# Two transformer blocks on one core: block one's attention heads computed by feature, sums and silu of block two placed elsewhere, other PSUM banks

## The reference

```python
mix = jnp.concatenate([y_m, y_b, y_n], axis=-1)          # 512 + 256 + 256 features
x = x + jnp.einsum('bse,ed->bsd', mix, w_out[l])
h = rmsnorm(x, norm_ffn[l])
u = jnp.square(jax.nn.relu(jnp.einsum('bsd,df->bsf', h, w_ff1[l])))
x = x + jnp.einsum('bsf,fd->bsd', u, w_ff2[l])
...
return gj[:, 0] * o_c + gj[:, 1] * o_s + gj[:, 2] * o_w   # nsa, per token and head
```

## Time and profile before

| | |
|---|---|
| median of 3 runs | 1090.6 us (1089.24 to 1091.53) |
| profiled execution, its time | 1088.39 us |
| its span | 1086.6 us |
| mean granted clock of TensorE | 0.997 of full |
| PE busy | 1064.1 us, 98% |
| DVE, ACT, POOL busy | 741.4, 618.6, 80.8 us |
| HBM read | 176.90 MB, 164 GB/s |

### The profile page before, as it was taken

One profiled execution on the slowest core, in us unless ns is written; L12 is line 12 of the kernel. 1 busy time (PEld: TensorE's weight loads), 2 busy tenths in 40 slices (PEclk: granted clock), 3 DMA queues, 4 the chain that ended last, 5 costly groups with the idle time before them and its releaser, 6 DMA issues.

```text
span 1086.6 us, 16764 instructions
## 1 busy us (share of the span) xinstructions
PE 1064.1 (98%) x6396; PEld 908.1 (84%) x6396; DVE 741.4 (68%) x1296; ACT 618.6 (57%) x1039; POOL 80.8 (7%) x96
## 2 busy tenths in 40 slices
PE   8999999999999999999999999999999999999997
PEld 7898888888888988888888887898987778989876
DVE  5889777677667888787766675684465657844554
ACT  6776754344436768563444354855656548556562
POOL 1010110000000100110000000004011000040120
PEclk9999999999999999999999999999999999999999
DMA  9853365555657534446566654654444456544432
GB/s 320 268 153 118 99 189 182 190 173 187 211 183 216 168 112 133 123 151 208 162 207 198 191 160 147 197 156 136 120 150 136 136 156 194 156 131 123 155 118 76
DMA packets 89404, 179.04 MB, mean 165 GB/s; under 512 B 8989, under 2 KB 20637, under 8 KB 89325
## 3 DMA queue, kind: packets, MB, share of 16 engines
q1 hardware_dynamic: 88605, 176.58, 52.1%
q10 hardware_dynamic: 720, 1.40, 0.4%
HBM read 176.90 MB, written 1.05 MB: 164 GB/s over the span
## 4 chain that ended last, share of the span: by engine, by line
PE 79%; DVE 8%; ACT 6%; issue 4%; DMA 3%; SPq 0%; DVEq 0%; POOL 0%; ACTq 0%; POOLq 0%
PE bank L852 18%; PE bank L854 17%; PE bank L853 17%; PE bank L918 11%; PE bank L920 5%; DVE w_lo L1824 2%; DMA raw<-in_w_in 2%; PE bank L1004 2%; ACT w_hi L1405 2%; PE bank L953 2%; PE bank L1061 1%; PE bank L1038 1%; DVE vecs L1833 1%; PE bank L1027 1%; PE bank L1333 1%
## 5 line engine op out<-in xcount | busy, mean ns | idle before, releaser
L1824 DVE TENSOR_TENSOR w_lo<-raw,w_hi 128x1024 fp32r<-128x1024 f32 (+1 forms) x319 | 385.7, 1221 | 228.1 <-ACT w_hi L1405 225.4
L1405 ACT ACTIVATE w_hi<-raw 128x1024 fp32r<-128x1024 f32 (+1 forms) x319 | 330.7, 1052 | 181.9 <-PE bank L854 96.7
L918 PE MATMUL bank<-h_parts,w_hi 128*128 128x512 f32 x512 | 180.7, 396 | 1.0 <-DVE arena L2201 0.7
L852 PE MATMUL bank<-h_parts,w_hi 128*128 128x256 f32 x512 | 149.3, 292 | 0.0
L853 PE MATMUL bank<-h_parts,w_hi 128*128 128x256 f32 x512 | 144.7, 283 | 0.0
L854 PE MATMUL bank<-h_parts,w_lo 128*128 128x256 f32 x512 | 144.6, 282 | 0.0
L852 PE MATMUL bank<-w_hi,h_parts 128*128 128x512 f32 (+1 forms) x352 | 141.2, 401 | 3.2 <-DVE w_lo L1866 2.0
L920 PE MATMUL bank<-h_parts,w_lo 128*128 128x256 f32 x512 | 143.4, 280 | 0.0
L853 PE MATMUL bank<-w_lo,h_parts 128*128 128x512 f32 (+1 forms) x352 | 136.5, 388 | 0.0
L854 PE MATMUL bank<-w_hi,h_parts 128*128 128x512 f32 (+1 forms) x352 | 136.5, 388 | 0.0
L918 PEld LDWEIGHTS bank<-h_parts,w_hi 128*128 128x128 f32 x512 | 96.0, 188 | 24.8 <-issue 2.6
(11 more groups left out here) (295 smaller groups left out, 1523.3 us busy)
## 6 DMA issues: line engine op xcount, KB each, us to landing
raw<-in_w_in SPq DMA_DIRECT2D x143, 512.0 KB, 3.8
raw<-in_w_ff SPq DMA_DIRECT2D x128, 512.0 KB, 4.3
raw<-in_w_out SPq DMA_DIRECT2D x40, 512.0 KB, 3.4
raw<-in_w_in SPq DMA_DIRECT2D x8, 404.0 KB, 5.5
xn<-in_cmp_w SPq DMA_DIRECT2D x8, 256.0 KB, 5.4
x_sb<-in_x SPq DMA_DIRECT2D x2, 512.0 KB, 9.1
mix<-in_cmp_w SPq DMA_DIRECT2D x4, 256.0 KB, 4.0
gain<-in_cmp_w SPq DMA_DIRECT2D x4, 256.0 KB, 5.6
```

The source lines that it names most:

```text
L852: pe.matmul(out_ap, s_hi, m_hi, start=start, stop=False, **kw)
L918: pe.matmul(ps[:, :].rearrange("p (a t) -> p a t", a=2), hi[:, kk, f], h_parts[:, :, k, :], start=k == 0, stop=False, skip_group_check=True)
L1405: act.activation(slot(w_hi, u), slot(raw, u), ACT.Copy).then_inc(hi_ready, 1)
L1824: dve.tensor_tensor(slot(w_lo, u), slot(raw, u), slot(w_hi, u).bitcast(F32), ALU.subtract)\
```

## The change

1. `BY_FEATURE` has "att1" too. In block one V runs once for a pair of heads, at the odd head's step, through `value_pair`; heads 0 to 3 accumulate in one use of bank 7, heads 4 to 11 in another. A stage N is added for each pair, at the end of step `start[h]` (the pair's S): DVE inverts the sums, times the gate for nsa (three instructions, two for moba); POOL scales the weights of both heads; T waits for POOL. `epilogue1` (three times a layer), the additions of its parts and `mix_turn` 2 and 3 are gone; after V of heads 3 and 11 ACT and DVE write `mixT1_hi`, `mixT1_lo` straight from bank 7.
2. `cmp_o` is computed transposed and added in bank 7; DVE's addition is gone.
3. Banks: the norms of the feed-forward use 4 to 7; `ff1(0)` uses banks 0, 1, 2, 4 and `ff1(1)` banks 5, 6, 7, 3.
4. The tail of the output projection waits for `mix_turn` 0 first and for `mix_turn` 1 only ahead of feature chunk 2.
5. Block two: `gate_silu` goes to the start of its step; `mix_full` to 33, 38, 48, 52; `mix_hi` to the start of 36, 39, 50, 53, and `mix_lo` one step after each; K of stick into the step of Z; the diagonal factor of the norm (L1885) from p = 5 to p = 4.

```diff
-BY_FEATURE = ("fox",)
+BY_FEATURE = ("att1", "fox",)
...
-        use(("norm", n, i, u), 2 * i if n in FFN_NORMS and u else 4 + 2 * u + i)
+        use(("norm", n, i, u), 4 + 2 * u + i)
...
-                for h in range(12):
+                for h in range(stage == "V", 12, 2 if stage == "V" else 1):
...
-                if p == 25:
-                    single(2, "mix_turn", 0, l, 2)
...
+                for h in range(0, 12, 2):
+                    if start[h] == p:
+                        head_steps(("att1", l), h, "N", 4)
...
-                use(("ff1", l, t, c), 4 + c)
+                use(("ff1", l, t, c), ((0, 1, 2, 4), (5, 6, 7, 3))[t][c] if t < 2 else 4 + c)
...
+            if p in (33, 48):
+                step("gate_silu", l, p // 48)
+            for n, turn_at in enumerate((36, 39, 50, 53)):
+                if p == turn_at:
+                    step("mix_hi", l, n)
+                if p == turn_at + 1:
+                    step("mix_lo", l, n)
...
-            for stage, lag in (("V", 3), ("R", 2), ("K", 1), ("Z", 0)):
+            for stage, lag in (("V", 3), ("R", 2), ("Z", 0), ("K", 0)):
...
+            if p in (33, 38, 48, 52):
+                step("mix_full", l, (33, 38, 48, 52).index(p))
...
+                    elif kind == "att1" and s[2] == "N":
+                        scale_weights("att1", l, s[3])
...
+                        elif s[2] == "N":
+                            g, r = divmod(s[3], 4)
+                            gate = n_gate[:, :, s[3]:s[3] + 2].rearrange("p i h -> p h i") if g else None
+                            row_inverses("att1", l, s[3], gate)
+                        elif s[2] == "V" and s[3] in (3, 11):
+                            g = s[3] // 8
+                            turned(("att1", l, "O", g), mixT1_hi[1][:, 2 * g:2 * g + 2, :], mixT1_lo[1][:, 2 * g:2 * g + 2, :])
```

More of the change, by code:

```diff
@@ L335, in hybrid_blocks @@
                 if p == 27:
-                    single(3, "cmp_o", l)
+                    step("cmp_o", l)
                     m_scores(0, 2)
@@ L351, in hybrid_blocks @@
             if p == 28:
-                single(7, "mix_turn", 0, l, 3)
                 m_values(0, 6)
@@ L429, in side2 @@
                 step("stats", 4 + l)
+            if p == 4:
+                step("r_diag", 4 + l)
             if p == 5:
@@ L933, in out_unit_products, with tail_products @@
                 return mm
-            def tail_products(name, a, features, turned_inside=()):
+            def tail_products(name, a, features, turned_inside=(), second_half=None):
                 for n, (f, hi_f, lo_f) in enumerate(features):
+                    if f == second_half:
+                        drained(pe, ("mix_turn", 0, name[2], 1))
                     if n < len(turned_inside):
@@ L1229, in _ @@
                         drained(pe, ("cmp_pT", l))
[L1230 to L1234, removed]
+                        ps = bank[bank_of["att1", l, "O", 1]]
+                        for c in range(2):
+                            pe.matmul(ps[:, c * T:(c + 1) * T], vc_diag[:, 2 * c:2 * c + 2, :].rearrange("p h d -> p (h d)"),
+                                      p_cmpT[:, :, :].rearrange("p i t -> p (i t)"), start=False, stop=False, skip_group_check=True)
                     elif kind == "mlstm" and s[2] == "S":
@@ L1258, in _ @@
                         pair = s[3]
[L1259 to L1264, removed]
+                        pe.wait_ge(mlstm_mixed, 2 * l + pair + 1)
                         turn(s, mix, [(2 * pair + c, i) for c in range(2) for i in range(NT)])
@@ L1268, in _ @@
                         if f % 2 == 0:
-                            drained(pe, ("mix_turn", 0, l, f // 2))
+                            drained(pe, ("att1", l, "O", f // 2 - 2) if f >= 4 else ("mix_turn", 0, l, f // 2))
                         finish_unit(out_unit_products(s, ("out", 0, l), mixT1_hi[f // 4][:, f % 4, :], mixT1_lo[f // 4][:, f % 4, :],
@@ L1272, in _ @@
                     elif kind == "tail" and s[1] == "out":
-                        drained(pe, ("mix_turn", 0, l, 1))
-                        tail_products(("out", 0, l), s[-1], [(f, mixT1_hi[0][:, f, :], mixT1_lo[0][:, f, :]) for f in (1, 2, 3)])
+                        drained(pe, ("mix_turn", 0, l, 0))
+                        tail_products(("out", 0, l), s[-1], [(f, mixT1_hi[0][:, f, :], mixT1_lo[0][:, f, :]) for f in (1, 2, 3)],
+                                      second_half=2)
                     elif kind == "tail":
@@ L1595, in _ @@
                         softmax_stage(kind, l, s[2], s[3])
+                        if s[2] == "V" and s[3] in (3, 11):
+                            g = s[3] // 8
+                            turned(("att1", l, "O", g), mixT1_hi[1][:, 2 * g:2 * g + 2, :])
                     elif kind == "mix_turn":
@@ L1953, in refine @@
                     tt(r, r, t, ALU.mult)
[L1955 to L1971, removed]
                 for s in timeline[0][l]:
@@ L2144, in _ @@
                         dve.tensor_tensor(pc, pc, seen_.unsqueeze(2).broadcast_to([P, NT, 4, NC_CMP]), ALU.mult).then_inc(cmp_ready, 1)
-                    elif kind == "cmp_o":
-                        dst = mix[:, :, 768:1024]
-                        free(dve.tensor_tensor(dst, dst, src(s)[:, :].rearrange("p (i c) -> p i c", i=NT), ALU.add), s)
                     elif kind == "mlstm" and s[2] == "S":
@@ L2162, in _ @@
                             free(dve.tensor_copy(probsT[:, s[3] % 3, :], ps[:, 0:384]), s)
-                        elif s[2] == "V" and s[3] % 4 == 3:
-                            epilogue1(s[3] // 4)
+                        elif s[2] == "N":
[3 more added lines that the diff above has]
+                        elif s[2] == "V" and s[3] in (3, 11):
+                            g = s[3] // 8
+                            turned(("att1", l, "O", g), mixT1_hi[1][:, 2 * g:2 * g + 2, :], mixT1_lo[1][:, 2 * g:2 * g + 2, :])
                     elif kind == "mlstm_end" and s[3] == 0:
@@ L2244, in _ @@
                         norm_step(*s[1:])
-                    elif kind == "r_row":
+                    elif kind == "r_diag":
                         factor_diag(s[1])
```

2 lines of the change are left out of this document (1 added, 1 removed).

## The result

The changed kernel takes 1105.1 us (median; 1103.91 to 1107.8) beside 1091.07 us for the kernel before in the same session: ratio 1.0135, 95% interval 1.0113 to 1.0158. It is 14 to 15 us slower. The prediction said slower, 1093.9 us, with a range that ended at 1098.5. Two of its sums held (block two, the hand-over to POOL), one was half of what it should have been: block one, +9.8 us for both layers where the chip shows about twice that.

The account below looks back on a forecast made before the run. PE, busy 98% of the span, was taken as the bound, with block one's DVE stretch deciding. Block one +9.8, block two -6.5 and feed-forward 0 gave +3.3 us on 1090.6: 1093.9 us, range 1087 to 1098.5.

Parts of the forecast that it names:

- block one, +9.8 us: Block one of both layers: each layer ends 4.5 us later, plus 0.4 us a layer for slowed DVE.
- DVE slowed under POOL's scaling: Block one: an allowance of 0.4 us a layer, bounds 0 and 2 us.
- PE saves 3.4 us a layer: Block one: V by pairs saves 2.5 us, two dropped `mix_turn` 0.9 us, if nothing is added before PE.
- T starts 1.9 us after N: Block one: POOL's first scaling is held until DVE's next `w_lo` ends; 0.9 us if not held.
- First meeting: Block one, p = 17: T of head 2 at 70.6 against 68.56, 2.05 us later.
- Second, T of head 6: Block one, p = 22: T of head 6 at 96.7, 4.5 us later; T of head 8 4.4 us late.
- Third, V of heads 8 and 9: Block one, p = 26: V waits 1.85 us and ends 1.1 us later relative to unit 25; 5.5 us late in all.
- Block two, -6.5 us: Block two: PE's waits for `mix_full` (4.4 us), K (1.6) and the diagonal factor (0.5) go; bounds -7 and -4.
- POOL is not held: Rival, block one: T follows N by 0.9 us, a layer ends 2.4 us later; 1088.9 us, chance 0.19.
- Covered: Rival: N and scaling end before PE reaches T everywhere, PE keeps its 6.8 us; 1077.3 us, chance 0.12.
- The moves in block two don't do it: Rival, block two: moved silus push T's copy and E, V of 4 and 5 waits 2 us; 1097.9 us, chance 0.05.
- DVE is held by POOL too: Rival, block one: POOL's scalings also hold DVE up, 2 us a layer; 1097.1 us, chance 0.14.

Follow-up runs that it names:

- e1_block_two: Kernel before plus the change's block-two moves and feed-forward banks, block one left by token; 1083.01 us, ratio 0.9939.
- e5_pool_beside: e1_block_two plus two POOL multiplications of 3x128 columns for each pair of heads, which nobody waits for; 1101.45 us, ratio 1.0108.
- e4_short_scaling: Changed kernel with every wait kept, but POOL multiplies only 3x8 of each block-one head's 3x128 columns; 1095.57 us, ratio 1.0048.
- e7_kept_warm: Changed kernel with 128x128 identity products on PE ahead of the wait for POOL at heads 2, 4, 6 and 8; 1097.87 us, ratio 1.0070.
- e3_exp_first: Changed kernel with a step's exponentials put ahead of the copies of T in ACT's queue; 1100.18 us, ratio 1.0100.
- e2_no_scaling: Changed kernel without N and without POOL's scaling in block one, T waiting for the exponentials only; 1079.62 us, ratio 0.9905.
- e9: Changed kernel with N kept on DVE and T waiting for its last instruction, no POOL scaling in block one; 1088.13 us, ratio 0.9981.
- e6: Changed kernel with block one's probabilities scaled by ACT after the exponentials' step instead of by POOL; 1095.48 us, ratio 1.0043.

## Why the prediction was half right

The direction and the mechanism (T waits for N and POOL behind DVE's queue) were right; the step that failed is the sum for block one, +9.8 us where the chip shows 21.4 (`e1_block_two` to the changed kernel). Three terms of it failed: DVE slowed under POOL's scaling, put at 0.4 us a layer; TensorE's clock after a stall, which has no term; and DVE's wait for the exponentials of heads 8 and 9, which has none either. The paragraphs below go through the sum in its order.

**What bounds the kernel** held: the stretch from p = 13 to 26, with DVE nearly unbroken, decides. What it understated is that DVE there is not covered by PE but level with it. `e5_pool_beside` shows it: 5 to 6 us more of DVE work, with nothing waiting for POOL, became 5.3 us of waits in layer 0, and with the clock behind them 10.3 us.

**PE saves 3.4 us a layer.** In matmuls yes: a pair's V goes from 78.18 to 78.98, the 0.80 us of the prediction. Realised without any chain were 3.7 us in both layers together, in part because PE then waits for `hid`.

**T starts 1.9 us after N.** Right: 1.85 us at head 2, 1.87 at head 6 (98.02 to 99.89), 1.88 at head 8 (108.94 to 110.82). That the first scaling stands behind `w_lo` is seen in the 1.31 us of `e4_short_scaling`.

**First meeting, 2.05 us.** Measured 2.9 after taking off the 0.9 us of the early wait. The missing 0.9 is the vector step of p = 14 under POOL's first pair, 3.7 us for 2.65. The step that failed begins here: "I add 0.4 us a layer for DVE slowed under POOL's scaling". Its bounds were 0 and 2 us. Summed over layer 0's block one, the same DVE instructions take 3.3 us more in the changed kernel than before: the convolutions 1.5, the vector step of p = 14 1.1, `hid` 0.6. The nearest row for it was one product of 0.55 us for 0.3, and I spread it over too few instructions and charged it to DVE alone; the queue has no slack to swallow it.

**Second, T of head 6, 4.5 us; T of head 8, 4.4 us.** Measured 6.8 and 9.3 us. Between the meetings two things were not in the sum at all. One is the clock: S of head 4 comes 1.6 us later because unit 18 runs partly at the lower level, and DVE's row maxima wait for it. `e7_kept_warm` puts the clock at 7.1 us at most of the whole kernel. The other is ACT's queue at p = 23: the prediction looked for "DVE waiting for ACT's exp only at N of head 10", and the first such wait is at N of head 8. `e3_exp_first` puts it at 3.8 us.

**Third, V of heads 8 and 9.** A wait of 1.85 us forecast, 1.54 measured. The rest of the layer gives back 0.7 us (forecast 1.0): late by 11.3 us behind this V (110.22 and 121.52), by 10.6 at `mix_turn` 0.

**Feed-forward, 0.** The wait moved as said, 0.34 us at `ff1(1)` for 0.40 us at the fourth accumulator, in layer 0. Beside it this stage is 0.4 to 0.8 us a layer longer in the changed kernel and in `e1_block_two` than before, with no wait in the list for it; its cause stays open.

**Block two, -6.5 us.** The gap to the kernel before falls from 22.7 us at the end of layer 1's feed-forward to 16.1 us at the end of the span, 6.6 us, with one window at the lower clock in it that the kernel before doesn't have; `e1_block_two` agrees with its 6.7.

**The rivals.** "POOL is not held" is out. "Covered" is out, and `e2_no_scaling`, 1079.6 us with no chain at all, shows that it could not have given its 1077.3. "The moves in block two don't do it" is out by `e1_block_two`. "DVE is held by POOL too" had 0.14 and 2 us a layer: it was the true one in kind, but its price was short (3.3 us a layer of DVE time, and what the waits and the clock make of it). The experiments don't split the 21.4 us of block one into shares that add without overlap: the ladder e2, e9, e4 splits it by links of the chain, e6, e3 and e7 by causes, and a DVE delay, a stall and a clock drop come of one another.

## What to carry over

When work goes to an idle engine, price first what it does to the engines it shares something with: here about 1.1 us of POOL a head, waited for by nobody, cost 18.4 us over 24 heads. An engine at 68% over the span can be the bound of the stretch in which the new work lands, so take its slack from the timeline of that stretch; where there is none, as here, each microsecond counts fully. And a stall of TensorE can cost more than its length, by what the clock takes afterwards: 1.6 us here for one of 2.80, and nothing for one of 2.79 a layer later. In a sum it is a bound for each stall, not a fixed price.

## What was not expected of the hardware

- A multiplication on POOL whose result nobody uses cost the kernel 18.4 us at 3x128 columns and none at 3x8.
- DVE's `TENSOR_SCALAR` on 30 columns, with one SBUF tensor as input, took 0.80 us beside POOL in place of 0.17: small instructions are held too. Of DVE's copies of 128x128, the one at 63.41 us of the changed kernel took 0.51 us in place of 0.23.
- After a stall of 2.80 us the granted clock fell (0.91 over 20 us) and matmuls of 256 columns started 0.21 us apart in place of 0.12, although they followed without a gap. With 128x128 products run during the wait it stayed at 1.00. Shorter waits did it too: in `e9_no_pool` waits of 1.00 and 0.91 us, 1.9 us apart, were followed by 0.50 from 72 to 74 us, and yet the wait of 2.79 us in layer 1 of the changed kernel was not followed by a drop. The page "TensorE: Matmul & The Clock Gate" of the Trainium skill, section "HAM oscillation — how this bites in real kernels", has idle gaps of the engine make its clock swing between the two levels; the windows of the changed kernel and of `e7_kept_warm` agree.
